# A fifth buffer for split weights, splits one piece further ahead, five summed pieces in every FFN, and new orders at the FFNs' ends

## What is computed

```python
for layer in range(2):                       # first block
    h = attention[layer](rms_norm(x, ...))   # neighbourhood, then dilated
    x = x + rms_norm(h, ...)
    h = (silu(n @ w_gate) * (n @ w_up)) @ w_down      # n = rms_norm(x, ...), d_ff = 2816
    x = x + rms_norm(h, ...)
for l in range(2):                           # second block
    x = x + 0.5 * swiglu_2(rms_norm_2(x, ffn1_norm[l]), ...)
    x = x + hybrid_mixing(rms_norm_2(x, mix_norm[l]), ...)
    x = x + 0.5 * swiglu_2(rms_norm_2(x, ffn2_norm[l]), ...)
```

## Time and profile before

| | |
|---|---|
| median of three runs | 1721.95 us |
| the profiled execution's own time | 1721.36 us |
| its span, first to last instruction | 1719.5 us |
| TensorE, matmuls | 99% busy, 10188 |
| TensorE, weight loads | 85% |
| VectorE | 83%, 2230 instructions |
| ScalarE | 61% |
| GpSimd | 7% |
| granted TensorE clock | full in all slices |
| weight queue (q1) | 312.55 MB, 50.3% of 16 engines |

### The profile page before, as it was taken

The page is one execution under the profiler, slowest core; times in us unless marked ns, Lnnn a source line. Parts: engine busy times, 40 slices in busy tenths (PEclk is TensorE's granted clock), DMA queues, the critical chain, the costliest instruction groups (busy, mean ns, idle before and its releaser), DMA issues.

```text
span 1719.5 us, 26116 instructions
## 1 busy us (share of the span) xinstructions
PE 1706.5 (99%) x10188; PEld 1469.0 (85%) x10188; DVE 1419.2 (83%) x2230; ACT 1053.7 (61%) x1681; POOL 114.1 (7%) x200
## 2 busy tenths in 40 slices
PE   9999999999999999999999999999999999999999
PEld 7888888788888888878888888888888888888887
DVE  5878888668886787969898888889888888889888
ACT  6666565555555665656566766666666657656653
POOL 1100000702220000000001110000000002000000
PEclk9999999999999999999999999999999999999999
DMA  8545546544443454645554344555465454436543
GB/s 324 189 164 201 191 172 231 207 172 164 154 167 140 157 203 163 232 180 180 196 173 183 140 170 172 200 193 184 183 215 187 166 195 172 148 147 214 192 178 127
DMA packets 45563, 314.83 MB, mean 183 GB/s; under 512 B 5072, under 2 KB 5584, under 8 KB 8448
## 3 DMA queue, kind: packets, MB, share of 16 engines
q1 hardware_dynamic: 45056, 312.55, 50.3%
q10 hardware_dynamic: 288, 0.52, 0.1%
q0 software_dynamic: 96, 0.10, 0.0%
HBM read 312.10 MB, written 1.05 MB: 182 GB/s over the span
## 4 chain that ended last, share of the span: by engine, by line
PE 81%; DVE 13%; DMA 3%; ACT 2%; issue 1%; SPq 0%; DVEq 0%; ACTq 0%
PE P L503 79%; DVE wl L2032 4%; DMA raw<-w_all 3%; ACT wh L1431 1%; PE P L516 1%; DVE hcv L2638 1%; PE P L899 1%; DVE fT L2249 1%; DVE xf L2233 1%; DVE xx L2249 1%; DVE xs L2253 1%; DVE xx L2067 0%; DVE fTf L2233 0%; DVE xs L2087 0%; DVE xf L2241 0%
## 5 line engine op out<-in xcount | busy, mean ns | idle before, releaser
L2032 DVE TENSOR_TENSOR wl<-raw,wh 128x2048 fp32r<-128x2048 f32 (+1 forms) x287 | 640.3, 2241 | 55.0 <-ACT wh L1431 51.2
L503 PE MATMUL P<-xx,wh 128*128 128x512 f32 (+2 forms) x2800 | 643.1, 384 | 0.0
L1431 ACT ACTIVATE wh<-raw 128x2048 fp32r<-128x2048 f32 (+2 forms) x290 | 538.0, 1858 | 101.4 <-DMA raw<-w_all 79.6
L503 PEld LDWEIGHTS P<-xx,wh 128*128 128x128 f32 (+1 forms) x2800 | 505.4, 188 | 96.7
L503 PE MATMUL P<-xx,wl 128*128 128x256 f32 x2688 | 350.8, 284 | 0.6 <-DVE nq L2495 0.6
L503 PEld LDWEIGHTS P<-xx,wl 128*128 128x128 f32 x2688 | 340.2, 191 | 11.2 <-DVE nq L2495 0.8
L1570 ACT ACTIVATE ft<-P 128x256 f32<-128x256 f32 x240 | 90.2, 382 | 212.2 <-PE P L503 212.2
L503 PE MATMUL P<-wh,xx 128*128 128x512 f32 x544 | 171.7, 395 | 0.0
L2205 DVE TENSOR_TENSOR fg<-P,ft 128x256 f32<-128x256 f32 x240 | 101.5, 423 | 78.2 <-ACT ft L1570 74.5
L503 PE MATMUL P<-wh,fhh 128*128 128x512 f32 x360 | 140.8, 391 | 0.0
L503 PE MATMUL P<-wl,fhh 128*128 128x512 f32 x360 | 140.1, 389 | 0.0
(11 more groups left out here) (397 smaller groups left out, 1979.6 us busy)
## 6 DMA issues: line engine op xcount, KB each, us to landing
raw<-w_all SPq DMA_DIRECT2D x289, 1024.0 KB, 4.8
nB<-rpb SPq DMA_DIRECT2D x4, 512.0 KB, 8.3
raw<-w_all SPq DMA_DIRECT2D x2, 512.0 KB, 6.8
xs<-x_in SPq DMA_DIRECT2D x1, 1024.0 KB, 7.4
fgb<-post SPq DMA_DIRECT2D x2, 512.0 KB, 5.5
out<-xs SPq DMA_DIRECT2D x4, 256.0 KB, 2.0
C<-cst SPq DMA_DIRECT2D x1, 775.0 KB, 6.5
ntm<-x_in ACTq DMA_DIRECT2D x2, 256.0 KB, 5.1
```

The costliest lines, as they stand in the source:

```text
L503: return t_.on.matmul(o, l, r, start=start, stop=stop, skip_group_check=True)
L1431: a.on.activation(o, i, ACT.Copy).then_inc(*hi.up((m,)))
L2032: v.on.tensor_tensor(o, i, h.bitcast(F32), ALU.subtract).then_inc(*lo.up(m))
```

## The change

- The ring of split buffers grows from 4 to 5. The memory comes from GpSimd's descriptor scratch, which shrinks to 256 bytes per partition; the loads of the `gu` weights therefore move to SP, behind the load of piece 7.
- In all FFNs ScalarE and VectorE split one piece further ahead: `ahead` gets an argument larger by one in the gate pieces and in the down projection.
- Stages 1 and 3 use FIVE: one more summed piece each, with its sums of h and its set of sums of weights.
- The ends of stages 1 and 3 get another order on VectorE: the split before `whole_last`, `whole_last` for the second half right behind the first half's x, and the split of the piece after next in two halves. TensorE waits for the halves of the piece concerned (HALVED).
- After the last summed piece the calls of `ahead` in the other stages are one less, so that they split the same piece as before there or none.
- In the mixer the first of the two low halves of L2865 moves up.

```diff
--- before.py
+++ after.py
@@ -18,7 +18,7 @@
 RAW = 3
-RING = 4
+RING = 5
@@ -43,8 +43,7 @@
 FIVE = Form("PSPSSPSSPPP", [(4, 5), (6, 7), (8, 9), (10, 11), (12, 13)], {0: 0, 1: 1, 2: 2, 4: 3, 5: 4}, (0, 1, 0, 1, 0))
-FOUR = Form("PSPSSPSPPPP", [(4, 5), (6, 7), (8, 9), (10, 11)], {0: 0, 1: 1, 2: 2, 4: 3}, (0, 1, 0, 1))
-FORM = {s: FOUR if s in (1, 3) else FIVE for s in (1, 3, 4, 6, 7, 9)}
+FORM = {s: FIVE for s in (1, 3, 4, 6, 7, 9)}
@@ -187,6 +186,7 @@
+HALVED = tuple(BASE[s + 1] + 2 for s in POST)
@@ -467,6 +467,10 @@
+                if m == RAW + 4:
+                    q.wait_ge(*gx.of("gu"))
+                    for r in (0, 32, 64):
+                        q.on.dma_start(AN["ngu"][r:r + 16, :, :], w_gu.rearrange("l k n -> k l n")).then_inc(*s_gu.up(0))
@@ -652,7 +656,7 @@
-                    t_.wait_ge(*(lo.of(0, i, hf) if m == 0 else lo.of(m)))
+                    t_.wait_ge(*(lo.of(0, i, hf) if m == 0 else lo.of(m, 2 * i // step) if m in HALVED else lo.of(m)))
@@ -1584,7 +1588,7 @@
                     if j:
-                        ahead(m + j + 2)
+                        ahead(m + j + 3)
@@ -1599,19 +1603,20 @@
-                        ahead(m + j + 3)
+                        ahead(m + j + 4)
...
                 for p in range(11):
...
-                    ahead(min(m + NF + p + 2, BASE[s + 1] - (1 if s in POST else 0)))
+                    if p != FORM[s].last:
+                        ahead(min(m + NF + p + 3, BASE[s + 1] - (1 if s in POST else 0)))
@@ -2120,8 +2125,6 @@
             def post_tile(s, t, gb, tmp, banks):
-                if s in FFNS and t:
-                    whole_last(s, t)
@@ -2145,22 +2148,26 @@
             def post_end(s, gb, tmp, banks):
 
                 m = BASE[s + 1]
+                ahead(m)
                 if s in FFNS:
                     whole_last(s, 0)
-                ahead(m)
-                if s not in TOK_FIRST:
+                else:
                     post_first(s, 0, gb, tmp, banks)
                 post_tile(s, 0, gb, tmp, banks)
-                if s not in TOK_FIRST:
+                if s in FFNS:
+                    whole_last(s, 1)
+                    turn(s + 1, 0, 0)
                     half_low(m + 2, 0)
...
+                    turn(s + 1, 0, 1)
+                    post_tile(s, 1, gb, tmp, banks)
+                    half_low(m + 2, 1)
...
-                else:
-                    ahead(m + 1)
-                post_tile(s, 1, gb, tmp, banks)
@@ -2281,7 +2288,7 @@
                 def sevens_down():
                     for p in range(11):
-                        n = m + NF + p + 2
+                        n = m + NF + p + 3
@@ -2290,9 +2297,9 @@
                         if p == FORM[s].last + 1:
                             sevens_first()
-                            ahead(n - 1)
+                            ahead(n - 2)
                             sevens_second()
-                            ahead(min(n, BASE[s + 1]))
+                            ahead(min(n - 1, BASE[s + 1]))
@@ -2677,12 +2684,14 @@
-                def short(f):
+                def short(f, between=None):
...
+                    if between is not None:
+                        between()
@@ -2853,16 +2862,23 @@
-                for f in range(2):
+
+                def square(f):
...
+                short(0)
+                square(0)
+                short(1, lambda: square_low(0))
+                square(1)
+                square_low(1)
@@ -2998,9 +3014,6 @@
-            g.wait_ge(*gx.of("gu"))
-            for r in (0, 32, 64):
-                g.on.dma_start(AN["ngu"][r:r + 16, :, :], w_gu.rearrange("l k n -> k l n")).then_inc(*s_gu.up(0))
@@ -3175,7 +3188,7 @@
-    nc = bacc.Bacc("TRN2", target_bir_lowering=False, num_devices=1)
+    nc = bacc.Bacc("TRN2", target_bir_lowering=False, num_devices=1, dynamic_dma_scratch_size=256)
```

More of the change, by code:

```diff
@@ L2147, in post_end @@
                 m = BASE[s + 1]
+                ahead(m)
                 if s in FFNS:
                     whole_last(s, 0)
-                ahead(m)
-                if s not in TOK_FIRST:
+                else:
                     post_first(s, 0, gb, tmp, banks)
                 post_tile(s, 0, gb, tmp, banks)
-                if s not in TOK_FIRST:
+                if s in FFNS:
+                    whole_last(s, 1)
+                    turn(s + 1, 0, 0)
                     half_low(m + 2, 0)
-                turn(s + 1, 0, 0)
-                turn(s + 1, 0, 1)
-                if s not in TOK_FIRST:
+                    turn(s + 1, 0, 1)
+                    post_tile(s, 1, gb, tmp, banks)
+                    half_low(m + 2, 1)
+                else:
+                    half_low(m + 2, 0)
+                    turn(s + 1, 0, 0)
+                    turn(s + 1, 0, 1)
                     post_first(s, 1, gb, tmp, banks)
                     half_low(m + 2, 1)
-                else:
-                    ahead(m + 1)
-                post_tile(s, 1, gb, tmp, banks)
+                    post_tile(s, 1, gb, tmp, banks)
                 turn(s + 1, 1, 0)
@@ L2855, in hybrid, with square_low @@
                 couple(hd[:, 4:6, :], m + 14, (3, 5), "hd2")
-                for f in range(2):
+                def square(f):
                     n = slice(f * S, (f + 1) * S)
-                    short(f)
                     v.wait_ge(*vh.of("sc", s, f))
                     v.on.tensor_tensor(Xd[:, n], c2[:, n], c2[:, n], ALU.mult).then_inc(*vh.up(("sqd", s, f)))
-                for f in range(2):
+                def square_low(f):
                     n = slice(f * S, (f + 1) * S)
```

## The result

The changed kernel takes 1762.07 us (median of 4 runs, 1761.44 to 1763.77) where the kernel before takes 1721.68 on the same chip: ratio 1.0236 (95% interval 1.0222 to 1.0249), 40.4 us slower. The forecast was 1744.8 with a range of 1731 to 1757: right in direction, 17 us short in size, and the measured time lies above the range. The profiled execution is the slowest of the four (1763.77, span 1762.0), so its sums come to 42.5 us against the span of 1719.5 before.

The account below looks back on a forecast made before the run. TensorE was taken to be at its own pace nearly everywhere, busy 1706.5 of 1719.5 us. Terms 2 x 4.05 + 3 x 3.9 + 3.2 - 0.2 = +22.8 us on the median 1721.95 gave 1744.8, range 1731 to 1757.

Parts of the forecast that it names:

- the two splits: Down projections: VectorE idles about 2 us before p4's split ahead of set 1 and p7's ahead of set 3.
- the sets: Stage 4's sets of sums 1 to 4: starts forecast at 878.1, 885.25, 895.8 and 902.95, in the earlier profile's times.
- The gathering sums: End of stage 4: VectorE's gathering operations, before at 908.66, come 6.1 us later, behind p10's split.
- The term of 3.2 us for T operands: Last summed piece of each of six FFNs: TensorE waits for late set 4, 2.9 us plus about 0.3.
- 0.3 us to ScalarE's: Each FFN: ScalarE's 1.9 us copy of p9 ahead of set 4's rounding adds about 0.3 us.
- The ends: Stages 1 and 3: each +4.05 us, as -0.7 + 3.8 + 2.15 - 1.2.
- The wait for xs: Ends of stages 1 and 3: TensorE waits 3.2 us where there were 1.05.
- the second one: Ends of stages 1 and 3: second xs wait, 1.45 us, goes; about 0.25 returns at the next stage's start.
- Rival 3: Loads issued back to back slow each other by 1.5 us: 3 us more per FFN, so 1763; chance 0.08.
- rival 1: Change works as it says: sums stay ahead of TensorE, ends lose their waits; -7.0 us, so 1715; chance 0.08.

Follow-up runs that it names:

- e13: Changed kernel, all orders kept, T-operand sums made from rounded weights so no load waits for a set of sums (products wrong, timing only): 1720.88 us.
- e5: Changed kernel with only VectorE's lookahead in the down projections put back as before, ScalarE's left as changed: 1764.39 us.
- e6: Changed kernel with only ScalarE's lookahead in the down projections put back as before, VectorE's left as changed: 1761.71 us.
- e8: The e2 kernel with 108 more matmuls of 512 columns put where TensorE waits (output wrong, timing only): 1748.58 us.
- e2: Changed kernel with the lookahead of before in the first two gate pieces of stages 1, 3 and 4 alone: 1757.04 us.
- e7: Changed kernel with old lookahead in down projections and at starts of stages 1, 3, 4, and one split moved at ends of stages 1, 3: 1715.20 us.
- e10: Against e7: four split buffers, the lookahead of before in the gate pieces too, and five raw buffers instead of three: 1714.83 us.
- e11: Against e7: at the ends of stages 1 and 3, low halves of the first transposes moved ahead of the moved split: 1719.09 us.
- e12: Against e7: four summed pieces in stages 1 and 3, as before, all else the same: 1716.42 us.
- e4: Changed kernel with 8 more matmuls of 512 columns in each FFN, meant for TensorE's waits (output wrong, timing only): 1758.47 us.

## Why the prediction was right in direction and short in size

**The mechanism.** VectorE was to idle 2.0 us before each of the two splits: 1.77 and 2.26. In stage 4, 23.15 us later than before (889.58 against 866.43), the sets were to start at 901.25, 908.40, 918.95 and 926.10; they start at 901.12, 908.26, 919.08 and 926.23. The gathering sums were to start at 937.95, and do at 937.92. The term of 3.2 us for T operands is 3.2 in stage 4 by the pitch (0.35, 1.86 and 1.03), 3.6 in stage 6, 3.7 in stages 3 and 9, 4.6 in stage 7 and 2.6 in stage 1. e13 shows that the hold on the raw buffers is behind it.

**Whose order.** The prediction gave the lateness to VectorE's order and 0.3 us to ScalarE's. e5 and e6 refute this split: with either order alone set 4 comes 5 to 6 us later than with both old ones (36.8 and 37.8 against 31.6), and the two overlap. The size of this term came out since VectorE's order is enough for it, but the remedy that it suggests, to mend VectorE's order, would have won nothing (e5). The rule that the prediction took from the Trainium skill (TensorE: Matmul & The Clock Gate, section on the array's architecture), that both engines' queues are strictly first in, first out, holds for ScalarE here as well: the trace of e5 agrees, with VectorE's 3.20 us of idle time for a rounding that stands behind ScalarE's copies. I had applied it to one of the two.

**The ends.** Forecast for stages 1 and 3 from the start of the down projection: 4.05 each; the rest columns give 5.1 - 1.1 = 4.0 and 6.5 - 1.5 = 5.0. The wait for xs was to be 3.2 us and is 3.8, the second one is gone, 0.3 came back at the next stage's start. All nine rests add to 24.5 against 22.8.

**The step that failed first: what a wait costs.** "The granted clock is full speed in the whole page" is true of the profile before, and I summed the new waits at full speed behind them. They were followed by seven half-clock stretches, 12.3 us; e8 shows that these go when TensorE has work in its waits. No rival held this.

**The step that failed second: an edit costed at nothing.** The longer lookahead in the gate pieces had no term ("VectorE idles in the gate pieces"). At the starts of stages 1, 3 and 4 TensorE waits 5.7 us for fhl in three places, and e2, which puts back the lookahead of both engines there, takes these away. In stage 1 ScalarE waits for a load ahead of a chain to TensorE (`ft` comes at 145.48, at 142.23 before), and VectorE then has one split more on it (4.49 us for two, 2.28 for one). How the 5.7 us divide between the two isn't shown, since no run changes one engine alone there. The trace of before has the warning: its one copy at that place already waited 3.36 us for its load.

Sum: 22.8 + 1.7 + 5.7 + 12.3 = 42.5. Rival 3 gave 1763 and was wrong all the same: its slow loads, 1.5 us longer each, aren't there. In stage 4 p4's load is issued at 893.14 and p7's at 911.01, each with the next one 0.42 us behind, and their copies start 4.8 and 4.9 us later; the median of all loads is 4.8 on both pages. That its number is the measured one is luck. Of rival 1's gain of 7.0 us, e7 gets 6.2, with the old lookahead in the down projections and at the starts and one split moved at the ends.

## What to carry to other kernels

Before splits or copies are moved ahead, list for each load what its buffer waits for; where that is a computation on an in-order engine, nothing that needs the load may stand ahead of that computation's successors, on any engine of the chain: mending one engine's order alone won nothing here. A deeper ring downstream gave 5 us here where it only covers late loads, and cost 35 where the lookahead that it allows crosses such a hold. And price new waits of TensorE with what the clock may take behind them: the changed kernel has nine places with 2.0 to 3.8 us of wait, 27.6 us together, and seven of them were followed by a half-clock stretch, 12.3 us in all.

## What the runs showed of the hardware that I had not expected

Behind waits of TensorE the granted clock falls to 0.50 (1.2 GHz) for stretches of 3.41 us, or twice that, and comes back by itself. In the sixteen profiles of this case there are 31, the double ones counted once and the last microseconds of each left aside, and each begins within a wait or at most 3 us behind it; the kernel before and e7, e8, e10, e11 and e12 have none. It isn't decided by a wait's length alone: in the changed kernel 3.0 us of waits in stage 6 were not followed by one, and 2.0 us in stage 1 were. e2, with nearly the same waits as the changed kernel in stages 4 and 6, got two there. In e6 each FFN has 2.9 us of waits at the same place, the last summed piece; in stages 1, 4 and 6 a stretch follows, in 3, 7 and 9 none. What decides between such cases I have not found. Where the matmuls put in took up the long wait, no stretch followed (e8, and stages 4, 6, 7 and 9 of e4). The Trainium skill (TensorE: Matmul & The Clock Gate, part on the clock gate) has it that the clock follows how busy TensorE has been of late; e8 agrees, with a mean of 1.000 over 1747.2 us, and no run here shows why equal waits differ.
